# Feed-forward of a transformer trunk in float32 on one NeuronCore: the last half chunk's gate and up projections in one weight tile, and activations awaited by chunk

## What is computed

```python
D_MODEL, D_FF, DEPTH = 1024, 2752, 2
def swiglu(h, wg, wu, wd):
    return (jax.nn.silu(h @ wg) * (h @ wu)) @ wd
def ffn_sub(h, m, sub, j, p):
    y = swiglu(sandwich_in(h, m, sub, p), p['w_gate'][j], p['w_up'][j], p['w_down'][j])
    return sandwich_out(h, y, m, sub, p, 0.5)
```

## Time and profile before

| | before |
|---|---|
| median of 3 runs | 3143.27 us (3143.07 to 3143.71) |
| profiled execution | 3142.62 us, span 3140.8 us, mean granted TensorE clock 0.974 |
| TensorE matmul | 2969.6 us busy, 95% |
| TensorE weight load | 2818.5 us, 90%, beside the matmuls |
| VectorE | 1650.3 us, 53% |
| ScalarE | 1022.6 us, 33% |
| GpSimd | 329.7 us, 10% |
| DMA | 299.73 MB, 95 GB/s over the span |

### The profile page before, as it was taken

How to read it: one execution, slowest core, us unless ns; L and a number is a source line. 1 busy time by engine, 2 the same in 40 slices (tenths; PEclk the granted TensorE clock), 3 DMA queues, 4 the chain that set the end, 5 groups by cost and what they waited for, 6 DMA issues and landing times. The chain is left out here.

```text
span 3140.8 us, 49298 instructions
## 1 busy us (share of the span) xinstructions
PE 2969.6 (95%) x18036; PEld 2818.5 (90%) x18036; DVE 1650.3 (53%) x2881; ACT 1022.6 (33%) x1718; POOL 329.7 (10%) x323
## 2 busy tenths in 40 slices
PE   6999999989898899999999999999998898899998
PEld 6999999979776889999999999999978776899997
DVE  4575666555246562555336575546556346643334
ACT  4212112443436452121224312212343435532233
POOL 2000000420003150000005000000230002500002
PEclk8999999999999999999999999999999999999999
DMA  7344344321200131344224344324432200433333
GB/s 232 114 126 133 108 133 128 111 80 54 61 15 31 57 98 56 93 133 127 61 68 119 108 130 127 101 87 135 113 91 57 80 5 27 135 88 100 92 89 114
DMA packets 456533, 299.73 MB, mean 95 GB/s; under 512 B 26254, under 2 KB 411636, under 8 KB 456380
## 3 DMA queue, kind: packets, MB, share of 16 engines
q1 hardware_dynamic: 453456, 291.01, 31.9%
q10 hardware_dynamic: 2924, 6.70, 0.6%
HBM read 295.33 MB, written 2.32 MB: 95 GB/s over the span
## 5 line engine op out<-in xcount | busy, mean ns | idle before, releaser
L1851 PE MATMUL ps<-hn,wsp 128*128 128x384 f32 (+1 forms) x3200 | 1051.1, 328 | 36.0 <-DVE hn L1386 19.9
L1852 PE MATMUL ps<-hn,wsp 128*128 128x384 f32 (+1 forms) x3200 | 1042.5, 326 | 0.0
L1853 PE MATMUL ps<-hn,wsp 128*128 128x384 f32 (+1 forms) x3200 | 1042.2, 326 | 0.0
L1298 DVE TENSOR_TENSOR wsp<-raw,wsp 128x1024 fp32r<-128x1024 f32 x368 | 456.3, 1240 | 501.3 <-ACT wsp L861 501.2
L1851 PEld LDWEIGHTS ps<-hn,wsp 128*128 128x128 f32 x3200 | 609.7, 191 | 50.2 <-issue 27.9
L1852 PEld LDWEIGHTS ps<-hn,wsp 128*128 128x128 f32 x3200 | 610.3, 191 | 0.0
L1853 PEld LDWEIGHTS ps<-hn,wsp 128*128 128x128 f32 x3200 | 609.9, 191 | 0.0
L861 ACT ACTIVATE wsp<-raw 128x1024 fp32r<-128x1024 f32 x408 | 429.4, 1052 | 508.7 <-PE ps L1853 502.2
L1851 PE MATMUL ps<-aT,wsp 128*128 128x384 f32 (+1 forms) x1408 | 458.8, 326 | 23.1 <-DVE aT L1476 19.3
L1852 PE MATMUL ps<-aT,wsp 128*128 128x384 f32 (+1 forms) x1408 | 454.5, 323 | 0.0
L1853 PE MATMUL ps<-aT,wsp 128*128 128x384 f32 (+1 forms) x1408 | 454.5, 323 | 0.0
(11 more groups left out here) (230 smaller groups left out, 2944.0 us busy)
## 6 DMA issues: line engine op xcount, KB each, us to landing
modw<-in_w_mod SPq DMA_DIRECT2D x144, 512.0 KB, 4.2
raw<-in_ffn_w_gate SPq DMA_DIRECT2D x192, 256.0 KB, 3.5
raw<-in_ffn_w_up SPq DMA_DIRECT2D x192, 256.0 KB, 4.1
raw<-in_ffn_w_down SPq DMA_DIRECT2D x64, 448.0 KB, 3.4
raw<-in_w_in SPq DMA_DIRECT2D x96, 256.0 KB, 3.1
raw<-in_ffn_w_down SPq DMA_DIRECT2D x64, 256.0 KB, 4.1
raw<-in_w_out SPq DMA_DIRECT2D x64, 256.0 KB, 3.2
raw<-in_ffn_w_down SPq DMA_DIRECT2D x64, 192.0 KB, 3.6
```

The source lines that it names most:

```text
L1298: dve.tensor_tensor(wsp[:, cs, 1, 0:width], raw[:, slot, 0:width], wsp[:, cs, 0, 0:width].bitcast(F32), ALU.subtract).then_inc(wlo_done, 1)
L1851: pe.matmul(dst, w(0), x(0), start=first, stop=False)
L1852: pe.matmul(dst, w(0), x(1), start=False, stop=False)
L1853: return pe.matmul(dst, w(1), x(0), start=False, stop=last)
```

## The change

- The last 64 hidden columns become a tile of their own: its columns 0 to 63 are the last 64 of gate, 64 to 127 the last 64 of up. One unit per half of the tokens makes both, gate in PSUM rows 0 to 63 and up in rows 64 to 127. There is one weight tile less per feed-forward, 79 instead of 80, so the parity of the tile numbers changes.
- SiLU reads PSUM rows 0 to 63 and writes rows 64 to 127 of its buffer. Product and high part work on rows 64 to 127; the low part is written to rows 0 to 63 of the high part's chunk.
- The down weights of this chunk hold the same 64 rows twice, in rows 0 to 63 and 64 to 127. So two matmuls (high weights, low weights) do what three did. The second copy is a third DMA per down tile of group 2, for which ACT waits on half_in. The zeroing of the rows and pad_done go.
- TensorE waits for activations by chunk: in the first down unit of a group for all but the last two chunks at block 0, for the chunk before the last at block G - 2, for the first half of the last chunk at block G - 1; for its second half at block G - 1 of the second unit, or in group 2 after the first pass.
- In the body of the half chunk there is one conversion less. The one that is left, of the second down tile, stands where the next gate tile's stood: on ACT behind both SiLUs, on DVE ahead of both products. It waits for both units of the half chunk.

The core of the diff:

```diff
@@ -153,7 +155,7 @@
 HEAD = 4
-FFN_TILES = HEAD + 2 * NCH + (len(GROUPS) + 1) * KD
+FFN_TILES = HEAD + 2 * NCH - 1 + (len(GROUPS) + 1) * KD
...
@@ -206,6 +208,13 @@
...
 def last_width(l, sub): return (KD if sub == 1 else GROUPS[-1][1]) * P
+def half_loads(t):
+    for f in range(2 * L):
+        i = t - last_tile0(f // 2, 2 * (f % 2))
+        if 0 <= i < 2 * KD:
+            return 2 * KD // RAW * f + i // RAW + 1
+    return 0
...
@@ -640,18 +651,35 @@
...
                     if g == len(GROUPS) - 1:
-                        up_body(0, [slice((NCH - 2) * P, (NCH - 1) * P), slice(LAST_F, FF)], mod_plan(l, j, g, UP_LAST))
-                        t0 += 4
+                        mod = mod_plan(l, j, g, UP_LAST)
+                        for s in range(3):
+                            at = (t0 + s) % RAW
+                            if s < 2:
+                                parts = cols_tile(at, (wg, wu)[s], slice((NCH - 2) * P, (NCH - 1) * P))
+                            else:
+                                dst = raw[:, at].rearrange("p (k f) -> p k f", f=P)
+                                parts = [(dst[:, :, w * HALF:(w + 1) * HALF],
+                                          (wg, wu)[w].rearrange("(k p) f -> p k f", p=P)[:, :, FF - HALF:FF])
+                                         for w in range(2)]
+                            load_tile(t0 + s, at, parts)
+                            if mod is not None:
+                                load_mod(mod[0], mod[0] // MOD_UNITS, mod[0] % MOD_UNITS, slice(s, s + 1 if s < 2 else 4))
+                        t0 += 3
...
                             cols = bass.ds((4 * i + s) * P, P)
+                            at = (t0 + s) % RAW
                             if g < len(GROUPS) - 1:
-                                parts = cols_tile(s, wd[c0 * P:(c0 + G) * P], cols, k=G)
+                                parts = cols_tile(at, wd[c0 * P:(c0 + G) * P], cols, k=G)
                             else:
-                                parts = [(raw[:, s, 0:(G - 1) * P].rearrange("p (k f) -> p k f", f=P),
+                                parts = [(raw[:, at, 0:(G - 1) * P].rearrange("p (k f) -> p k f", f=P),
                                           wd[c0 * P:(c0 + G - 1) * P].rearrange("(k p) f -> p k f", p=P)[:, :, cols]),
-                                         (raw[:, s, (G - 1) * P:G * P], wd[LAST_F:FF, cols])]
-                            load_tile(t0 + 4 * i + s, s, parts)
+                                         (raw[0:HALF, at, (G - 1) * P:G * P], wd[FF - HALF:FF, cols])]
+                            load_tile(t0 + 4 * i + s, at, parts)
+                            if g == len(GROUPS) - 1:
+                                sp.dma_start(raw[HALF:P, at, (G - 1) * P:G * P], wd[FF - HALF:FF, cols]
+                                             ).then_inc(half_in[at], 16)
...
@@ -856,6 +884,8 @@
...
                 act.wait_ge(raw_in[slot], 32 * nth)
+                if isinstance(t, int) and half_loads(t):
+                    act.wait_ge(half_in[slot], 16 * half_loads(t))
...
@@ -957,22 +987,26 @@
...
                         for b in range(2):
-                            t = t0 + 4 * i + 2 * b
+                            half = last and b == 1
+                            lo = OVER if half else 0
...
                                 act.wait_ge(amul_done, q + n + 1)
-                                act.activation(sg2[n][:, 0:w], ps[:, n, 0:w], ACT.Silu).then_inc(silu_done, 1)
-                            w_hi(t + 2, (s + 2) % RAW, 0, (t0 + 2 * b + 2) // RAW + 1 + i, used + 2)
+                                act.activation(sg2[n][lo:P, 0:w], ps[0:P - lo, n, 0:w], ACT.Silu).then_inc(silu_done, 1)
+                            w_hi_in_loop(i, s + 2, used + 2)
...
                                 act.wait_ge(amul_done, q + n + 3)
-                                lo = OVER if last and b == 1 else 0
...
                                                ).then_inc(ahi_done, 1)
-                            w_hi(t + 3, (s + 3) % RAW, 1, (t0 + 2 * b + 3) // RAW + 1 + i, used + 4)
+                            if not half:
+                                w_hi_in_loop(i, s + 3, used + 4)
+                    def w_hi_in_loop(i, s, used):
+                        w_hi(t0 + 4 * i + s, (t0 + s) % RAW, (t0 + s) % 2, (t0 + s) // RAW + 1 + i, used)
...
@@ -1470,11 +1503,12 @@
...
                     dve.wait_ge(alo_done, q + 1)
-                    dve.tensor_tensor(af2[b][:, 0:w], ps[:, bank, 0:w], sg2[b][:, 0:w], ALU.mult
+                    dve.tensor_tensor(af2[b][lo:P, 0:w], ps[lo:P, bank, 0:w], sg2[b][lo:P, 0:w], ALU.mult
...
                     dve.wait_ge(ahi_done, q + 1)
-                    dve.tensor_tensor(aT[lo:P, 1, kc, a:a + w], af2[b][lo:P, 0:w],
-                                      aT[lo:P, 0, kc, a:a + w].bitcast(F32), ALU.subtract).then_inc(alo_done, 1)
+                    low = aT[0:HALF, 0, kc, a:a + w] if lo else aT[:, 1, kc, a:a + w]
+                    dve.tensor_tensor(low, af2[b][lo:P, 0:w], aT[lo:P, 0, kc, a:a + w].bitcast(F32), ALU.subtract
+                                      ).then_inc(alo_done, 1)
...
@@ -1489,28 +1523,26 @@
...
                 for g, (c0, G) in enumerate(GROUPS):
+                    def w_lo_in_loop(i, s):
+                        w_lo(t0 + 4 * i + s, (t0 + s) % RAW, (t0 + s) % 2)
...
                         for b in range(2):
-                            t = t0 + 4 * i + 2 * b
+                            half = last and b == 1
...
                             s = 2 * b
-                            used = units_before(t0) + 8 * i + 4 * b + 2
+                            used = units_before(t0) + 8 * i + 4 * b + (0 if half else 2)
...
                                 mod_tiles(mod[0] + i, (2 * b, 2 * b + 1))
-                            w_lo(t + 2, (s + 2) % RAW, 0)
+                            w_lo_in_loop(i, s + 2)
                             for n, (a, w) in enumerate(hv):
-                                activated(q + n, n, k0 + 2 * i + b, a, w, 2 + n, used + n + 1,
-                                          OVER if last and b == 1 else 0)
-                            w_lo(t + 3, (s + 3) % RAW, 1)
+                                activated(q + n, n, k0 + 2 * i + b, a, w, n if half else 2 + n, used + n + 1,
+                                          OVER if half else 0)
+                            if not half:
+                                w_lo_in_loop(i, s + 3)
...
-                    if g == len(GROUPS) - 1:
-                        dve.wait_ge(unit_done, units_before(t0))
-                        for half in range(2):
-                            ins = dve.memset(aT[0:OVER, half, G - 1].bitcast(F32), 0.0)
-                        ins.then_inc(pad_done, 1)
...
@@ -1913,11 +1945,17 @@
...
-            def output(bank, cs, G, a, w, x, ready=None):
+            def output(bank, cs, G, a, w, x, ready=None, half=False):
...
                         ready(k)
+                    if half and k == G - 1:
+                        for p in range(2):
+                            ins = pe.matmul(ps[:, bank, 0:w], weight(cs, k * P)(p), x[0][:, k, a:a + w],
+                                            start=False, stop=p == 1)
+                        continue
...
@@ -1940,11 +1979,19 @@
...
                     return
-                pe.wait_ge(alo_done, ffn_pair0(l, sub // 2) + 2 * NCH + 2)
-                pe.wait_ge(pad_done, 2 * l + sub // 2 + 1)
+                q = ffn_pair0(l, sub // 2) + 2 * NCH
...
                     for s in range(4):
-                        last_output(l, sub, 0, 4 * i + s, s)
+                        last_output(l, sub, 0, 4 * i + s, s, active(q, GROUPS[-1][1], 0) if s == 0 else None)
+                pe.wait_ge(alo_done, q + 2)
+            def active(q, G, n):
+                def ready(k):
+                    late = {0: 4, G - 2: 2, G - 1: 1} if n == 0 else {G - 1: 0}
+                    if k in late:
+                        pe.wait_ge(alo_done, q + 2 - late[k])
+                return ready
...
@@ -1993,15 +2040,15 @@
...
                 for g, (c0, G) in enumerate(GROUPS):
-                    def up_body(i, first, mod):
+                    def up_body(i, first, mod, last=False):
...
                             q = q0 + 4 * i + 2 * b
-                            for wi, freed in ((0, silu_done), (1, amul_done)):
+                            for wi, freed in ((0, silu_done), (1, amul_done))[:1 if last and b else 2]:
...
                                     pe.wait_ge(freed, q + 1 + max(n, first))
-                                    output(2 * wi + n, wi, KD, a, w, hn2)
+                                    output(2 * wi + n, (t0 + wi) % 2, KD, a, w, hn2)
...
@@ -2023,9 +2070,7 @@
...
                                 pe.wait_ge(yadd_done, d0 + 8 * i + 2 * s + n + 1)
-                                if s == 0 and n == 0:
-                                    pe.wait_ge(alo_done, q0 + 2)
```

(19 more changed lines are left out.)

7 lines of the change are left out of this document (3 added, 4 removed).

## The result

| | before | after |
|---|---|---|
| median of the comparison's runs | 3143.49 us (3143.07 to 3144.08, 4 runs) | 3102.84 us (3101.42 to 3106.74, 4 runs) |
| profiled execution | 3142.62 us, span 3140.8 us | 3106.74 us, span 3104.9 us |
| granted TensorE clock, mean | 0.974 | 0.971 |

The time after is 0.9873 of that before (95% interval 0.9855 to 0.989): 40.7 us less, where the prediction's sum was 49.8. The profiled executions lie 35.9 us apart, since the one of after is the longest of its four.

The account below looks back on a forecast made before the run. TensorE, busy 95% of the span, was taken as the bound. 30.6 + 15.0 + 1.6 - 2.8 + 5.4 = 49.8 us off the profiled 3142.62 gave 3092.8, plus 0.65 for the median 3093.5 us; range 3086 to 3104.

Parts of the forecast that it names:

- rival 2: Group 2: new stalls lower the clock at all four boundaries, tails hide everything; 3103.3 us, chance 0.10.
- Part A: Half chunk: four units of 24 matmuls become two, 48 matmuls fewer per feed-forward; 30.6 us gained.
- Part B: Groups 0 and 1: waits by chunk remove TensorE's stall at eight boundaries; 14.96 us gained.
- Part D: Down units of group 2, first passes and tails: one matmul fewer per unit; 5.4 us gained.
- the clock of FFN 1.1: First boundary of FFN 1.1: without the stall the low clock goes; 1.6 us back, bounds 0 and 1.6.
- part C: Group 2: conversion ahead of the activations delays the third down unit; together -2.8 us, bounds +9 and -9.
- Part E: Down tile loads: third DMA, ACT's extra wait for it, load order and changed tile parity cost nothing.
- Rival 1: Half chunk: the order costs nothing, third down unit starts at 8.0 or 8.8 us; 3081.7 us, chance 0.09.
- Rival 3: Last passes: third DMA makes the tile load the bound; at 15.2 us, 58 us lost, 3151 us; chance 0.03.
- Rival 4: Half chunk: its matmuls are not fewer on the chip, so no change; 3143.3 us, chance 0.02.

Follow-up runs that it names:

- e5_best: e3_both with the gcol steps one chunk earlier, where DVE is idle: 3083.57 us, ratio 0.9813 to the kernel before.
- e4_fill: The changed kernel with ten matmuls, result unread, between second and third down unit, TensorE's tile loop written out: 3092.71 us, ratio 0.983 to the kernel before.
- a1_again: The changed kernel once more, unedited: 3101.95 us, ratio 0.9869 to the kernel before.
- e1_order: The changed kernel with the half chunk's activations ahead of the second down tile's conversion, on ACT and DVE: 3089.88 us, ratio 0.982 to the kernel before.
- e3_both: The changed kernel with e1_order's edit, gcol steps ahead of the half chunk's mod tiles, mod_reduce behind the last pass's first conversion: 3084.35 us, ratio 0.9806.

## Why the prediction was right, and where it was off

The time, 3102.84 us, lies in the range (3086 to 3104) near its upper end, 9.3 us above the forecast and 0.5 us from rival 2's 3103.3. The sign held, and so did parts A, B and D, which make most of the gain. In group 2, rival 2 was nearer than the forecast: the clock did fall behind the new stalls. That its time fits so well is in part luck: it has 4.9 us too little lost in group 2 (9 against 2.8 + 3.3 + 7.8), and 3.7 us too little gained in part D and at the clock of FFN 1.1.

- **Part A**: right, and seen by itself: from the first up unit of group 2 to S, after takes 8.32 us less at 384 columns and 5.68 less in FFN 1.1, 30.6 us in all, and 256 matmuls are gone. The table's second row, 24.5 us, is this less part C's 2.8 and the 3.3 that part C had too little (below).
- **Part B and the clock in FFN 1.1**: right, 16.6 us for 16.55. No gap is left at a boundary of groups 0 and 1, and the low clock of the earlier trace rows went with its stall.
- **Part C**: the mechanism was right, its size was not. The third unit starts at S + 12.7, 11.4, 12.7 and 9.7, where I had 11.8, 10.6, 11.8 and 9.0: 3.3 us in all. The steps are each as long as taken; missing are handovers. ACT begins the conversion 0.51 us after SiLU instead of 0.4 (542.15 - 541.64), DVE has 0.41 us between gcol steps and evacuation, and some 0.03 us lie between every two steps. The wait inside the first unit of FFN 0.1 is 1.18 us, where I had 1.2; the waits for the low half are two, of 1.0 and 1.7 us, where I had about four. mod_turn in FFN 0.0 and 1.0 waits 0.4 us for mod tiles that end at S + 0.5. Part C had this very number and called it no new wait; it is one, but off the chain that sets the third unit.
- **The low clock behind the new stalls**: left out of the sum, and the largest error, 7.8 us. Rival 2 had it at all four places at 1.6 us each, and said "against: stalls of 2.45 us at 384 columns had none". That comparison failed, since it took the group boundaries alone. The trace of before has the clock fall at other waits, in norms and mixers. Here are two of them, each with the busy time by stretch behind it (columns as in the earlier trace rows):

```profile
703.28 0.79 PE L1851 MATMUL ps<-wsp,hn 128*128 128x512 f32 x1 [2.87 <-DVE wsp L1298]
703.20:706.20 3.00, 2.92 (x7) 2.34 (x8) 2.96 (x3) 2.96 (x4) 0.00 (x0) 0.50 0.59 164
...
2310.01 0.88 PE L1866 MATMUL ps<-cst,scr 128*128 128x1 f32 x6 [1.89 <-POOL scr L746]
2310.60:2314.00 3.40, 3.40 (x14) 3.40 (x14) 0.18 (x1) 1.12 (x2) 0.00 (x0) 0.50 0.35 129
```

Take TensorE's waits in that trace that begin at the full clock after some 10 us of nearly unbroken work, by the idle time in the row. A low stretch began in the wait or up to 2 us behind it at 0 of 12 waits of 1.2 to 1.8 us, at 5 of 12 of 1.8 to 2.4 us, and at 10 of 10 of 2.7 us and more. The new waits are idle for 3.05 us (FFN 0.0 and 1.0), 1.95 (0.1) and 2.12 (1.1). So zero was not the price even at the length that follows from part C's own steps for FFN 0.0 and 1.0: mod_turn from S + 0.5 on and two units end at 0.5 + 0.79 + 2 x 3.99 = 9.3, 2.5 us ahead of the third unit's 11.8. Rival 2's other half, tails that hide everything, did not happen, nor did its zero for the clock in FFN 1.1.

- **Part D**: right, 5.6 us for 5.4. From the third down unit to the tail, the low clock's price set aside, a 384-wide FFN gives 1.04 to 1.05 us (forecast 1.04) and FFN 1.1 0.37 (0.36); the tails give 0.51 and 0.57 (0.5 and 0.4).
- **Part E**: no wait on a down tile's load appears; DVE, not a DMA, ends every wait for a third unit. Rivals 1, 3 and 4 didn't occur. Rival 1's 8.0 for the third unit is near what the exchanged order gives in FFN 0.1 (S + 8.5 in e5_best); its 8.8 for FFN 0.0 and 1.0 is not reached, 10.0 is. Rival 3's example was misreckoned: four times 3.4 is 13.6 us and not 15.2, below its own bound of 14.3, so it lacked even that basis.
- The Trainium skill ("TensorE: Matmul & The Clock Gate", section "What's actually happening") has the low rate as the gate's default, released by activity. That side of it, a new stall that lowers the clock, agrees with e4_fill: with work in the stall the granted clock stays at 1.00, 2.4 GHz.

Adding up: 49.8 - 3.3 - 7.8 + 0.2 = 38.9 us, within 2 us of the medians' 40.7; the profiled execution is 2.9 us short of it, about what two executions of the same kernel differ by in one stretch.

## What to carry to other kernels

When a wait is cut out of the engine that bounds, write down the queue of each engine that feeds it for the next two units: a step that becomes due earlier (here a tile's conversion, whose slot is freed later than before) must not stand ahead of the work that the bounding engine wants first. Price a new stall of TensorE as its length plus a chance of half rate behind it, and take that chance from all waits in the trace of before, not only from those of the same kind; here the half rate added 1.5 to 2.9 us where it happened. Two parts of a change can be worth more together than apart (16.7 us against 5.3 and 5.3 around the last chunks), so judging one alone may reject both.

## What the runs showed of the hardware

- Waits and the clock. All ten traces without their first 45 us (the changed kernel is in them twice), TensorE's waits that begin at the full clock after some 10 us of nearly unbroken work, by the idle time in the row, with those at or up to 2 us behind which a low stretch began:

| idle time, us | waits | with a low stretch |
|---|---|---|
| 1.2 to 1.8 | 88 | 0 |
| 1.8 to 2.4 | 78 | 42 |
| 2.7 to 3.5 | 65 | 58 |
| over 3.5 | 44 | 44 |

- At the third down units: idle for 3.05 us (FFN 0.0 and 1.0, after and a1_again), low in four of four; 1.95 and 2.12 us (FFN 0.1 and 1.1, the same kernels), low in three of four; 1.70 us (FFN 0.0 and 1.0, e1_order), none; ten matmuls in the wait and 1.24 us or less left idle (e4_fill), none. The 1.95 and 2.12 us follow an earlier wait, inside the first unit; that this matters is not shown, since single waits of that length go either way.
- The same kernel at the same wait had the low clock in one execution and not in the other, and for 3.4 us once and 6.8 us another time, so it is to be priced as a chance.
- Ten matmuls whose result is thrown away, 1.7 us of TensorE's time in a stall, made the unit behind it faster by 1.5 to 2.6 us. It is a probe and a stopgap: e3_both, which shortens the stall itself, took 3084.35 us against 3092.71 on the same chip, with no execution in common; e1_order's 3089.88 overlaps with it.
